# Differential attention: maps turned three blocks behind their scores, the maximum written negated, and the rotation's rows exchanged by transfers instead of matmuls

## The reference, cut to what matters

```python
def project(h, rotate):
    q, k, v = jnp.split(h @ w_in, 3, axis=-1)
    q = q.reshape(B, T, H, 2, d) * (d ** -0.5)        # H = 8 heads, two maps each, d = 64
    k = k.reshape(B, T, H, 2, d)
    if rotate:                                         # latent tokens only
        q, k = _apply_rope(q, cos, sin), _apply_rope(k, cos, sin)
    return q, k, v.reshape(B, T, H, 2 * d)

def _apply_rope(x, cos, sin):                          # halves of 16 rows: x1, x2
    out = stack([x1 * c - x2 * s, x2 * c + x1 * s])

def attend(q, k, v):
    s = jnp.einsum('bqhjd,bshjd->bhjqs', q, k).astype(jnp.float32)
    p = jax.nn.softmax(s, axis=-1)
    a = (p[:, :, 0] - lam_full * p[:, :, 1]).astype(v.dtype)
    o = jnp.einsum('bhqs,bshe->bqhe', a, v)
    return _rms(o) * subln_g * (1.0 - lam_init)
```

## Time and profile before

| | us |
|---|---|
| median of 3 runs | 1935.22 |
| profiled execution | 1935.05 |
| its span | 1933.4 |
| TensorE busy | 1893.6 (98%) |
| VectorE busy | 1143.6 (59%) |
| ScalarE busy | 665.9 (34%) |
| GpSimd busy | 136.5 (7%) |
| value projection, about | 492.8 to 547.1 |
| attention, about | 549 to 641 |

### The profile page before, as it was taken

The page is one execution under the profiler, slowest core; times in us unless marked ns, Lnnn a source line. Parts: engine busy times, 40 slices in busy tenths (PEclk is TensorE's granted clock), DMA queues, the critical chain, the costliest instruction groups (busy, mean ns, idle before and its releaser), DMA issues.

```text
span 1933.4 us, 29212 instructions
## 1 busy us (share of the span) xinstructions
PE 1893.6 (98%) x10896; PEld 1659.1 (86%) x10896; DVE 1143.6 (59%) x1858; ACT 665.9 (34%) x1052; POOL 136.5 (7%) x196
## 2 busy tenths in 40 slices
PE   8999999999989999999999999999999999999998
PEld 6888888898955898888889888888898998989998
DVE  7887772263468478777424777752362534655554
ACT  5322322242257343223223322232243322544442
POOL 0001000000001211000000110100100000010000
PEclk9999999999989999999999999999999999999999
DMA  8466543244210136666332566633343220545554
GB/s 314 157 209 193 184 151 104 90 129 138 88 44 1 45 111 214 195 196 183 103 106 88 178 207 194 195 106 105 92 153 126 93 87 22 175 153 174 185 164 129
DMA packets 80861, 269.75 MB, mean 140 GB/s; under 512 B 8977, under 2 KB 14353, under 8 KB 80785
## 3 DMA queue, kind: packets, MB, share of 16 engines
q1 hardware_dynamic: 62354, 201.58, 32.0%
q0 software_dynamic: 18432, 67.12, 11.4%
HBM read 267.62 MB, written 1.05 MB: 139 GB/s over the span
## 4 chain that ended last, share of the span: by engine, by line
PE 92%; DVE 5%; issue 1%; DMA 1%; ACT 0%; SPq 0%; POOL 0%; POOLq 0%; DVEq 0%; ACTq 0%
PE pt L1267 23%; PE pt L1270 23%; PE pt L1268 23%; PE pt L1393 3%; PE pt L1502 2%; PE pt L1503 2%; PE pt L1504 2%; PE pt L1629 2%; PE pt L1631 2%; PE pt L1630 2%; PE pt L1569 1%; PE pt L1397 1%; PE pt L1333 1%; PE pt L1535 1%; DVE wl L774 1%
## 5 line engine op out<-in xcount | busy, mean ns | idle before, releaser
L774 DVE TENSOR_TENSOR wl<-raw,wh 128x1024 fp32r<-128x1024 f32 (+2 forms) x394 | 432.4, 1137 | 511.7 <-ACT wh L542 507.8
L1267 PE MATMUL pt<-xh,wh 128*128 128x512 f32 (+1 forms) x1632 | 584.9, 358 | 0.2 <-DVE wl L774 0.2
L1268 PE MATMUL pt<-xh,wl 128*128 128x512 f32 (+1 forms) x1632 | 584.1, 358 | 0.0
L1270 PE MATMUL pt<-xl,wh 128*128 128x512 f32 (+1 forms) x1632 | 582.7, 358 | 0.0
L542 ACT CAST wh<-raw 128x1024 fp32r<-128x1024 f32 (+2 forms) x394 | 364.1, 970 | 243.9 <-PE pt L1270 188.8
L1270 PEld LDWEIGHTS pt<-xl,wh 128*128 128x128 f32 x1632 | 308.3, 189 | 45.0
L1268 PEld LDWEIGHTS pt<-xh,wl 128*128 128x128 f32 x1632 | 308.4, 189 | 44.9
L1267 PEld LDWEIGHTS pt<-xh,wh 128*128 128x128 f32 x1632 | 308.4, 189 | 44.9 <-issue 0.3
L786 DVE CUSTOM_DVE_ANT_0 pt<-modw,raw 128x1024 f32<-128x1024 f32 x256 | 305.7, 1255 | 10.8 <-DMA modw<-in_mod_rows 10.8
L1267 PE MATMUL pt<-uh,wh 128*128 128x512 f32 (+1 forms) x572 | 203.9, 356 | 0.0
L1268 PE MATMUL pt<-uh,wl 128*128 128x512 f32 (+1 forms) x572 | 203.9, 356 | 0.0
(11 more groups left out here) (186 smaller groups left out, 2308.4 us busy)
## 6 DMA issues: line engine op xcount, KB each, us to landing
raw<-in_ffn_w SPq DMA_DIRECT2D x238, 512.0 KB, 4.0
modw<-in_mod_rows POOLq DMA_DIRECT2D x128, 512.0 KB, 4.6
raw<-in_ret_w_in SPq DMA_DIRECT2D x48, 512.0 KB, 4.4
raw<-in_diff_w_in SPq DMA_DIRECT2D x24, 512.0 KB, 4.3
raw<-in_ffn_w SPq DMA_DIRECT2D x32, 256.0 KB, 3.9
raw<-in_ret_w_out SPq DMA_DIRECT2D x16, 512.0 KB, 4.1
region<-in_mod_rows SPq DMA_DIRECT2D x8, 512.0 KB, 14.6
region<-in_mod_start SPq DMA_DIRECT2D x8, 512.0 KB, 15.2
```

Source lines behind the costliest of these rows:

```text
L774: nc.vector.tensor_tensor(flat(wl[:, s, cut]), raw[:, raw_slot(late, s, p), 0:part_rows * CW], flat(wh[:, s, cut].bitcast(F32)), ALU.subtr ...
L1267: nc.tensor.matmul(bank, w_hi[:, k, cut], hi(k), start=a, stop=False)
L1268: nc.tensor.matmul(bank, w_lo[:, k, cut], hi(k), start=False, stop=False)
L1270: return nc.tensor.matmul(bank, w_hi[:, k, cut], lo(k), start=False, stop=b)
```

## The change

1. In `diff_v`, the 16 permutation matmuls and TensorE's waits around them are gone. Instead GpSimd, once all of q and k is copied out, issues 32 transfers from SBUF to SBUF: for each of four groups of four tiles, eight transfers of 16 partitions each, into a new tile `other_rows` (which lies where the exponentials and turned maps of the attention will lie later). `rope(r)` waits for its group's eight transfers and reads `other_rows` instead of PSUM.
2. `copy_out` multiplies q by 1/8 while copying; the exponentials lose their scale, and the maximum is written negated by the reduction itself, so that the small multiply behind it and its semaphore are gone. ScalarE's loop over four pairs becomes two loops over two.
3. In `diff_attn` the turn of a block comes three steps behind its score instead of two (`TURN_LAG = 3`), on TensorE and in ScalarE's copy. The values and all per-head steps move one step later with it. VectorE's order of mixtures and maxima stays.
4. A wait that GpSimd did twice is done once.

```diff
--- before.py
+++ after.py
@@ -35,8 +35,10 @@
 LAM_INIT = 0.8 - 0.6 * float(np.exp(np.float64(0.0)))
 V = 4 * DH
-AT_SUM, AT_SPREAD = 9, 11
-AT_SQUARE, AT_HI, AT_LO = 7, 12, 13
+
+TURN_LAG = 3
+AT_SUM, AT_SPREAD = TURN_LAG + 7, TURN_LAG + 9
+AT_SQUARE, AT_HI, AT_LO = TURN_LAG + 5, TURN_LAG + 10, TURN_LAG + 11
 V_STEPS = 4 * (DH - 1) + AT_HI + 1
 RH = 4
 RK = 256
@@ -240,6 +242,8 @@
         aTd = part(2, TT, LAT)
         orawd = part(DH, TOK)
         droped = part(2, LAT)
+
+        other_rows = part(2 * DH, LAT, at=taken[0] - 2 * LAT - DH * TOK - 2 * TT * LAT - 4 * TOK)
         qr = part(DT, LAT, at=0)
         kr = part(DT, TOK)
         vr = part(TT, 2 * D)
@@ -284,6 +288,7 @@
         unit_ready = sem("unit_ready")
         start_landed = [sem(f"start_landed{d}") for d in range(DT)]
         x_landed = [sem(f"x_landed{g}") for g in range(4)]
+        swap_landed = [sem(f"swap_landed{g}") for g in range(4)]
         start_piece_landed = [sem(f"start_piece_landed{n}") for n in range(4)]
         cond_spread, start_folded = sem("cond_spread"), sem("start_folded")
         start_made, start_step, start_shifted = sem("start_made"), sem("start_step"), sem("start_shifted")
@@ -294,7 +299,7 @@
         lam_step, lam_exp = sem("lam_step"), sem("lam_exp")
         rope_landed, swapped, rope_terms, roped = (sem("rope_landed"), sem("swapped"), sem("rope_terms"),
                                                    sem("roped"))
-        scored, topped, shifted, exped = sem("scored"), sem("topped"), sem("shifted"), sem("exped")
+        scored, shifted, exped = sem("scored"), sem("shifted"), sem("exped")
         ratio_ready, mixed, probs_turned, probs_ready = (sem("ratio_ready"), sem("mixed"), sem("probs_turned"),
                                                          sem("probs_ready"))
         mass_squared = sem("mass_squared")
@@ -502,9 +507,6 @@
                     if u0 == START_UNITS:
                         pool.wait_ge(lo_ready, 4)
-                    if u0 == START_UNITS:
-
-                        pool.wait_ge(lo_ready, 4)
                     for e in range(2):
                         fetch(u0, e, u0 // (MODT // 2))
                     for L in range(DEPTH):
@@ -514,6 +516,15 @@
                             with pool.Fori(a, b) as u:
                                 for e in range(2):
                                     fetch(u, e, L)
+                if kind == "diff_v":
+
+                    for s in range(2):
+                        pool.wait_ge(evac[s], 2 * (ph["sa"], ph["sb"])[s])
+                    n = DD // 4
+                    for g in range(4):
+                        for b in range(P // n):
+                            pool.dma_start(other_rows[b * n:(b + 1) * n, 4 * g:4 * g + 4, :],
+                                           qk[(b ^ 1) * n:((b ^ 1) + 1) * n, 4 * g:4 * g + 4, 0:LAT]).then_inc(swap_landed[g], 16)
                 if kind == "down":
                     clear(ph)
                     for e in range(POOLED):
@@ -554,11 +565,12 @@
                     act.wait_ge(evac[half], 2 * (before[("sa", "sb")[half]] + 2 - half) + t + 1)
                     act.wait_ge(sq_added, (1 + POOLED) * (ph["n"] - 1) + POOLED + t)
                     square(POOLED + t, slice(half * LAT, (half + 1) * LAT))
-            def copy_out(ph, dst, T, i, s):
+            def copy_out(ph, dst, T, i, s, factor=1.0):
                 for t in range(2):
                     tile_done((ph["sa"], ph["sb"])[s] + i, s, t, 2 * (ph["q"] + i) + s)
-                    nc.scalar.copy(row(dst, 4 * i + 2 * s + t)[:, 0:T], pt[:, 2 * s + t, 0:T]).then_inc(evac[s], 1)
+                    nc.scalar.activation(row(dst, 4 * i + 2 * s + t)[:, 0:T], pt[:, 2 * s + t, 0:T], ACT.Copy,
+                                         scale=factor).then_inc(evac[s], 1)
                 split(ph["q"] + i + 1, s, late=is_late(ph))
             def decay_logs():
                 act.wait_ge(g_step, 1)
@@ -680,7 +692,12 @@
                         for s in range(2):
                             copy_out(ph, dst, T, 1, s)
                         continue
-                    with act.Fori(0, (2 if kind != "diff_qk" else 4)) as i:
+                    if kind == "diff_qk":
+
+                        with act.Fori(0, 2) as i:
+                            for s in range(2):
+                                copy_out(ph, dst, T, i, s, factor=DD ** -0.5)
+                    with act.Fori(2 if kind == "diff_qk" else 0, 4 if kind == "diff_qk" else 2) as i:
                         for s in range(2):
                             copy_out(ph, dst, T, i, s)
                 elif kind in ("diff_v", "ret_v"):
@@ -706,7 +723,7 @@
                         if u >= 2:
                             act.wait_ge(probs_turned, 2 * (u - 2) + b + 1)
                         for j in range(2):
-                            nc.scalar.activation(ex(u, b)[:, j, 0:nk], pt[:, 2 * b + j, 0:nk], ACT.Exp, scale=DD ** -0.5,
+                            nc.scalar.activation(ex(u, b)[:, j, 0:nk], pt[:, 2 * b + j, 0:nk], ACT.Exp,
                                                  bias=shift[:, 2 * b + j:2 * b + j + 1],
                                                  accum_out=masses(u, b)[:, j:j + 1]).then_inc(exped, 1)
                     def turn_out(u, b):
@@ -726,8 +743,8 @@
                         act.wait_ge(o_scaled, h + 1)
                         nc.scalar.copy(xh[:, h, :], tmp[:, 2 + h % 2, :]).then_inc(o_hi, 1)
                     for v in range(V_STEPS):
-                        if 2 <= v < V + 2:
-                            turn_out((v - 2) // 2, v % 2)
+                        if TURN_LAG <= v < V + TURN_LAG:
+                            turn_out((v - TURN_LAG) // 2, (v - TURN_LAG) % 2)
                         if v < V:
                             exps(v // 2, v % 2)
                         for at, step in ((AT_SQUARE, square_o), (AT_HI, hi_o)):
@@ -1101,8 +1118,8 @@
                         decay_products(0)
                         decay_products(1)
                     def rope(r, bank, tile):
-                        dve.wait_ge(swapped, r + 1)
-                        nc.vector.tensor_tensor(tmp[:, bank % 2, 0:LAT], pt[:, bank, 0:LAT], droped[:, 1], ALU.mult).then_inc(rope_terms, 1)
+                        dve.wait_ge(swap_landed[r // 4], 16 * P * 4 // DD)
+                        nc.vector.tensor_tensor(tmp[:, bank % 2, 0:LAT], other_rows[:, r, :], droped[:, 1], ALU.mult).then_inc(rope_terms, 1)
                         nc.vector.tensor_tensor(tile, tile, droped[:, 0], ALU.mult).then_inc(rope_terms, 1)
                         dve.wait_ge(rope_terms, 2 * r + 2)
                         nc.vector.tensor_tensor(tile, tile, tmp[:, bank % 2, 0:LAT], ALU.add).then_inc(roped, 1)
@@ -1138,10 +1155,8 @@
                     def row_max(u, b):
                         nk = TOK if u % 2 == 0 else CTX
                         dve.wait_ge(scored, 2 * u + b + 1)
-                        nc.vector.tensor_reduce(top[:, 2 * b:2 * b + 2], pt[:, 2 * b:2 * b + 2, 0:nk], AX.X, ALU.max).then_inc(topped, 1)
-                        dve.wait_ge(topped, 2 * u + b + 1)
-                        nc.vector.tensor_scalar(shift[:, 2 * b:2 * b + 2], top[:, 2 * b:2 * b + 2], -(DD ** -0.5), None,
-                                                ALU.mult).then_inc(shifted, 1)
+                        nc.vector.tensor_reduce(shift[:, 2 * b:2 * b + 2], pt[:, 2 * b:2 * b + 2, 0:nk], AX.X, ALU.max,
+                                                negate=True).then_inc(shifted, 1)
                     def mix(u, b):
                         nk = TOK if u % 2 == 0 else CTX
                         v = 2 * u + b
@@ -1489,12 +1504,6 @@
                         for s in range(2):
                             pe.wait_ge(lo_ready, 2 * (2 * (q0 + i) + s + 1))
                             claim(s, s0[s] + i, 1)
-                            for e in range(4 if diff else 0):
-                                r = 8 * i + 4 * s + e
-                                if not (first and s == 0):
-                                    pe.wait_ge(roped, r - 3)
-                                nc.tensor.matmul(pt[:, 4 + e, 0:LAT], swap_d, row(qk, r)[:, 0:LAT], start=True,
-                                                 stop=True).then_inc(swapped, 1)
                             for n in range(TT):
                                 at = pt[:, 2 * s + n // 2, (n % 2) * CW:(n % 2 + 1) * CW]
                                 cut = slice(n * P, (n + 1) * P)
@@ -1541,10 +1550,10 @@
                     for v in range(V_STEPS):
                         if 0 < v < V:
                             score(v // 2, v % 2)
-                        if 2 <= v < V + 2:
-                            turn_probs(v // 2 - 1, v % 2)
-                        if 4 <= v < V + 4 and v % 2 == 0:
-                            values(v // 2 - 2)
+                        if TURN_LAG <= v < V + TURN_LAG:
```

(3 more changed lines are left out.)

## The result

| | before | after |
|---|---|---|
| median | 1935.34 us (4 runs) | 1915.81 us (4 runs) |
| profiled execution | 1935.05 | 1916.37 |
| its span | 1933.4 | 1914.7 |

The ratio is 0.990, 95% interval 0.9883 to 0.9918: 19.5 us faster. Forecast were 1917.0 us and a range of 1914.5 to 1927.0.

What follows compares the result with a forecast made beforehand. TensorE, busy 98% of the span, was taken as the bound. From 1935.05 us, 6.9 for the projection's matmuls and 11.1 for the attention (8.2 idle, 2.9 clock) came off, transfers costing nothing: 1917.0 us, range 1914.5 to 1927.0.

Steps and rivals of the forecast that it cites:

- The projection: Value projection: removing the exchange matmuls from TensorE takes 1.73 us off each of four chunks, 6.9 us.
- The exchange: GpSimd's 32 transfers before the attention: issued 0.56 us apart, overlapping, hidden with over 20 us to spare, cost nothing.
- The attention: Attention: a later turn closes TensorE's waits; 8.2 us of idle time plus 2.9 of clock, 11.1 us off.
- the allowance of 1.0 for hand-overs: Attention: 1.0 us taken off the 9.2 us of removed idle time, for hand-overs a walk through one head doesn't see.
- the multiply: Attention, VectorE: dropping the small multiply behind each maximum saves about 0.1 us each on VectorE; nothing taken in the sum.
- the slow start: Attention's start: clock 0.50 at 555 to 557 us follows an idle time that stays; left in, no gain taken.
- The two drops in the heads: Attention: granted clock of 0.86 in one head and 0.84 in the last stretch would go, 2.9 us.
- The condition put on the clock: Attention: TensorE's clock taken to stay at 2.4 GHz once the waits are gone, worth 2.9 us.
- case B: Rival, attention: score-maximum-exponentials alternation and VectorE's order bound it; only the multiply saves, 0.2 us a head: 1926.5 us; chance 0.14.
- D: Rival, behind the attention: saved time is waited for again, for weights or modulation columns, leaving 1935 us; chance 0.03.

Runs made afterwards that it cites:

- matmuls back: Changed kernel with the rows exchanged by the 16 permutation matmuls again, no transfers, `rope` reading PSUM: 1922.30 us (0.9933).
- transfers alone: Kernel before with only the transfers and the factor in the copies; TURN_LAG = 2, plain maximum, small multiply and its wait kept: 1928.96 us (0.9968).
- turn two behind: Changed kernel with TURN_LAG = 2 instead of 3, transfers and negated maximum kept: 1923.72 us (0.9943).
- multiply back: Changed kernel with the maximum written plainly and the small multiply by -1 and its wait behind it, TURN_LAG = 3 kept: 1919.13 us (0.9918).
- fourth step: Changed kernel with TURN_LAG = 4 instead of 3: 1917.93 us (0.9911).
- pieces at 14, 18: Changed kernel with the split of the output projection's second weight chunk moved from before the attention's first exponentials and mixture to its steps 14 and 18: 1915.26 us.
- pieces at 6, 10: Changed kernel with the split of the output projection's second weight chunk moved from before the attention's first exponentials and mixture to its steps 6 and 10: 1913.21 us.
- idle multiply: Changed kernel with TURN_LAG = 2, negated maximum kept, plus a small multiply of constants behind each maximum that nobody needs: 1925.04 us (0.995).

## Why the prediction was right, and where its terms were off

**The projection**: right. 1.73 us a chunk, 6.9 us in all, shown by the chunk of 11.51 us and by the run with the matmuls (6.5). In the traces the projection ends 7.3 us earlier; the 0.4 above 6.9 lies within the 539.5 to 541.0 us at which it ends in the kernels with the transfers not held back.

**The exchange**: right that it is hidden; the issues took 512 ns (0.56 taken). The first group landed later than forecast, at 504.4 instead of 500 to 503: four weight loads ran beside it and the slowest landing was 6.7 us. It had until 509. The lock-out that the Trainium skill speaks of doesn't show: the longest of 32 issues is 541 ns, with VectorE busy 4.05 of 11.51 us beside them. The page ties it to a two-port mode, and the trace doesn't say in which mode VectorE's splits and rotations ran, so this shows that they don't delay the issues, and is no test of the rule.

**The attention**: 11.1 us forecast, 13.65 measured. The mechanism was right: the order on TensorE closes the idle time. The whole attention in the traces, with the time that it ran at half clock (read in steps of 0.25 us):

| kernel | length | TensorE busy | idle | at half clock |
|---|---|---|---|---|
| before | 93.86 | 80.59 | 13.27 | 17.1 |
| transfers alone | 93.81 | 80.59 | 13.22 | 17.1 |
| turn two behind | 87.05 | 76.28 | 10.77 | 6.8 |
| multiply back | 82.54 | 77.59 | 4.95 | 10.2 |
| matmuls back | 80.82 | 77.09 | 3.73 | 10.2 |
| changed | 80.21 | 75.97 | 4.24 | 6.8 |
| fourth step | 81.64 | 75.49 | 6.15 | 6.8 |
| pieces at 14, 18 | 78.70 | 74.98 | 3.72 | 3.4 |
| pieces at 6, 10 | 77.50 | 73.48 | 4.02 | 0 |

The transfers alone and the multiply back differ in nothing but the turn's distance. The order alone gives 93.81 - 82.54 = 11.3 us: 8.3 of idle time and 3.0 of clock, where the prediction took 8.2 and 2.9. So the terms that it counted came out to 0.1 us each, the allowance of 1.0 for hand-overs included. What it lacked is the multiply, taken at nothing: with it gone too, 0.7 us more of idle time go, and the slow start, which was to be left in, is 6.8 us long instead of 10.2 (1.6 us). The idle time can be put down to the multiply, by what two traces of the changed kernel leave of it; the clock can't, since the matmuls back have the long slow start without it. The two drops in the heads are gone, as forecast.

**The condition put on the clock was too strict.** The prediction let the clock stay up "once the waits are gone". With the turn two behind TensorE still waits 7.9 us for mixtures, in 13 places, and keeps 0.88 us of idle time a head, and no head has a drop; with the idle multiply it is about 1.0 us a head, and again no drop. The transfers alone, at 1.29, have the drops of the kernel before. Less idle time went with fewer drops, but it need not be none.

**The multiply was sized too small**, as 0.2 us a head in case B and as nothing in the sum. At a turn two behind it and its wait are worth 93.81 - 87.05 = 6.8 us: 2.5 of idle time (0.4 a head) and 4.3 of clock. At a turn three behind they are worth 2.3 us at most, and by idle time alone 0.3 to 0.7 (a second trace of the changed kernel idles 4.66 us). The failing step was to take its cost from how far its own interval reached beyond its neighbours' (0.1 us), when the wait ahead of it also cut the overlap with the reduction. Case B is refuted, since the order did close the gaps; with the multiply's real price its number would have been the 1923.7 of the run with the turn two behind. The two parts overlap: the order is worth 11.3 us beside the multiply and 6.8 without it.

**D was half there.** TensorE reached the output projection 640.99 - 620.06 = 20.9 us earlier, but the span fell by 18.7. The last VectorE instructions stand 20.4 us apart in the two traces:

```profile
L923 DVE SCALAR_TENSOR_TENSOR region<-hT,cols_in,pt x8: 473/473/480, 1927.1 to 1929.9; 128x256 f32<-128x256 f32 x8
```

```profile
L940 DVE SCALAR_TENSOR_TENSOR region<-hT,cols_in,pt x8: 476/476/481, 1906.7 to 1909.4; 128x256 f32<-128x256 f32 x8
```

The other 1.7 us are after them, where only the stores are left. They aren't an accident of this execution: they are the 1.2 to 1.8 us that every kernel with the transfers shows there and the run with the matmuls back doesn't. So time is given back, though not in waits for weights or modulation columns, where D looked for it. The medians are 19.5 us apart. That 1917.0 came so near to 1915.8 is partly luck: the forecast had 2.6 us too little for the attention, and nothing for what is lost behind it, and the two misses cancel in part.

## What to carry to other kernels

When two engines alternate on a chain, read the idle time of the one that bounds the rest of the kernel, and ask whether its next independent work can stand ahead of the instruction that waits; one step was worth 11 us here while VectorE also carried the multiply, 7 us without it, and a second step cost 1 at the start. Price an instruction that is pipelined by what it adds on the chain, not by its duration, and an instruction that waits for its own engine by the start-to-start time with and without it. A transfer that has 43 us to land can go out in 32 small pieces, as long as they overlap. And when a stage gains more than the whole, follow the difference to where it is lost, in more than one trace.

## What was not expected of the hardware

A wait of VectorE for its own reduction costs 0.13 us, beside the 0.07 of the instruction behind it (1.34, 1.21 and 1.14 us from reduction to reciprocal). And the clock drop in the middle of the attention comes back in the run with the transfers alone, in a head of the same 12.13 us that begins, counted between spreads, 53 us after the projection's end in both, though that end is 6 us earlier. So what the engines did before it seems to have a part in it. It is not all: in the 26 runs of the kernel before beside the experiments the mean granted clock goes from 0.990 to 0.993, and the 11 runs at 0.993 took 1931.2 to 1935.1 us, the 14 at 0.990 or 0.991 took 1934.9 to 1936.5. The same program has more slow stretches in one execution than in another. Nor was it expected that kernels with the 32 transfers end 1.2 to 1.8 us later behind their last VectorE instruction.
